# Columns of the activation tiles in SBUF, and the first weight panel of an encoder step

## The reference

```python
for l in range(DEPTH):
    hn = rmsnorm(x, p['norm_mix_pre'][l])
    m = mixer_even(hn, ...) if l % 2 == 0 else mixer_odd(hn, ...)
    x = x + rmsnorm(m, p['norm_mix_post'][l])
    hn = rmsnorm(x, p['norm_ffn_pre'][l])
    f = jnp.square(jax.nn.relu(hn @ p['mlp_up'][l])) @ p['mlp_down'][l]
    x = x + rmsnorm(f, p['norm_ffn_post'][l])
```

## Time and profile before

| | |
|---|---|
| median of 3 runs | 2187.01 us (2185.21 to 2187.84) |
| the profiled execution | 2186.56 us |
| its span, first to last instruction | 2184.6 us |
| TensorE busy | 2168.7 us, 99% |
| VectorE busy | 907.4 us, 42% |
| ScalarE busy | 666.8 us, 31% |
| TensorE's granted clock over the span | 0.998 |

### The profile page before, as it was taken

One profiled execution on the slowest core, in us unless ns is written; L12 is line 12 of the kernel. 1 busy time (PEld: TensorE's weight loads), 2 busy tenths in 40 slices (PEclk: granted clock), 3 DMA queues, 4 the chain that ended last, 5 costly groups with the idle time before them and its releaser, 6 DMA issues.

```text
span 2184.6 us, 31823 instructions
## 1 busy us (share of the span) xinstructions
PE 2168.7 (99%) x13629; PEld 2154.2 (99%) x13629; DVE 907.4 (42%) x1431; ACT 666.8 (31%) x1137; POOL 96.3 (4%) x115
## 2 busy tenths in 40 slices
PE   9999999999999999999999999999999999999998
PEld 8999999999999999999999999999999999999997
DVE  5766358323322322334953333493223223322336
ACT  6664345202311320333511112453013103202333
POOL 1000000000000000000033231000000000000000
PEclk9999999999999999999999999999999999999999
DMA  6111422111111111132311114221111111111132
GB/s 218 49 41 39 138 75 83 49 47 41 49 49 49 41 48 49 49 110 67 119 49 41 47 49 138 69 81 56 49 42 47 49 49 47 41 49 49 55 122 80
DMA packets 228891, 142.99 MB, mean 65 GB/s; under 512 B 5248, under 2 KB 227408, under 8 KB 228752
## 3 DMA queue, kind: packets, MB, share of 16 engines
q1 hardware_dynamic: 228304, 140.89, 21.3%
q0 software_dynamic: 416, 0.07, 0.0%
q10 hardware_dynamic: 32, 0.01, 0.0%
HBM read 119.22 MB, written 21.73 MB: 65 GB/s over the span
## 4 chain that ended last, share of the span: by engine, by line
PE 88%; DVE 2%; issue 0%; ACT 0%; DVEq 0%; ACTq 0%
PE ps L679 29%; PE ps L680 29%; PE ps L682 29%; DVE x_lo L1383 1%; DVE x_old L1372 0%; DVE f L1355 0%; PE ps L781 0%; DVE f L1339 0%; DVE f L1347 0%; DVE f L1365 0%; DVE w_all L1306 0%; PE ps L719 0%; DVE f L1434 0%; ACT tmp L945 0%; PE ps L804 0%
## 5 line engine op out<-in xcount | busy, mean ns | idle before, releaser
L679 PE MATMUL ps<-x_hi,w_all 128*128 128x352 f32 x2328 | 757.6, 325 | 1.5 <-DVE x_lo L1383 1.5
L680 PE MATMUL ps<-x_lo,w_all 128*128 128x352 f32 x2328 | 748.5, 322 | 0.0
L682 PE MATMUL ps<-x_hi,w_all 128*128 128x352 f32 x2304 | 740.3, 321 | 0.0
L679 PE MATMUL ps<-h_hi,w_all 128*128 128x352 f32 x1728 | 556.5, 322 | 0.0
L682 PE MATMUL ps<-h_hi,w_all 128*128 128x352 f32 x1728 | 555.2, 321 | 0.0
L680 PE MATMUL ps<-h_lo,w_all 128*128 128x352 f32 x1728 | 555.2, 321 | 0.0
L679 PEld LDWEIGHTS ps<-x_hi,w_all 128*128 128x128 f32 x2328 | 437.5, 188 | 5.4 <-issue 2.0
L680 PEld LDWEIGHTS ps<-x_lo,w_all 128*128 128x128 f32 x2328 | 437.6, 188 | 2.2
L682 PEld LDWEIGHTS ps<-x_hi,w_all 128*128 128x128 f32 x2304 | 432.6, 188 | 0.0
L909 ACT CAST w_all<-w_all_raw 128x1024 fp32r<-128x1024 f32 x168 | 175.5, 1045 | 522.1 <-DMA w_all_raw<-in_mlp_down_dram 317.8
L679 PEld LDWEIGHTS ps<-h_hi,w_all 128*128 128x128 f32 x1728 | 324.4, 188 | 0.4 <-DVE h_lo L1595 0.3
(11 more groups left out here) (218 smaller groups left out, 1458.0 us busy)
## 6 DMA issues: line engine op xcount, KB each, us to landing
w_all_raw<-in_mlp_up_dram SPq DMA_DIRECT2D x60, 512.0 KB, 3.9
w_all_raw<-in_mlp_down_dram SPq DMA_DIRECT2D x60, 512.0 KB, 3.9
x_save<-f SPq DMA_DIRECT2D x12, 1408.0 KB, 6.4
x_old<-x_save SPq DMA_DIRECT2D x12, 1408.0 KB, 11.5
w_all_raw<-in_c_w_in_dram SPq DMA_DIRECT2D x22, 512.0 KB, 3.8
w_all_raw<-in_w_in_even_dram SPq DMA_DIRECT2D x15, 512.0 KB, 3.8
x_rows<-in_x_prompt_dram SPq DMA_DIRECT2D x8, 512.0 KB, 7.5
w_all_raw<-in_w_out_even_dram SPq DMA_DIRECT2D x6, 512.0 KB, 3.9
```

The source lines that it names most:

```text
L679: nc.tensor.matmul(dst, wh, hi, start=(i == 0), stop=False)
L680: nc.tensor.matmul(dst, wh, lo, start=False, stop=False)
L682: last = nc.tensor.matmul(dst, wl, hi, start=False, stop=(i == KC - 1))
```

## The change

1. A chunk of x now has 1152 columns (`XS`), and its tiles stand 384 columns apart (1536 bytes, six times 256) with a gap of 32 columns behind each. All three tiles of x begin at the same place within 256 bytes, the one where tile 0 was. Tiles of h stay as they were.
2. The buffer `sq_sum` goes. Its 352 columns a tile lie in the gaps of x, as 11 pieces of 32 columns; so do `fold`, `root`, `rcol` and, in 4 pieces a row, `tail_rows`. VectorE's operations on them take the pieces in one instruction each.
3. `rstd` now stands behind `tmp` and is what the warm-up reads. Room that `sq_sum` gave is taken by what shared it: `bias_bc`, `v_tok_s` and `row_junk` lie on `tmp`; `xc1` and `ig1` lie in chunks 1 and 2 of `h_lo`, the scratch `v_junk` and `v_out_s` in chunk 3. So in `spatial_bias` the wait for the recurrence's last product and gates comes before step 3 and not 6, the wait for the output of v before step 9 and not 3, and `out_sum` waits for neither `v_out` nor `t_out`.
4. The first panel is loaded in two transfers, chunks 0 to 3 and 4 to 7. VectorE casts chunks 0 to 3; ScalarE casts chunks 4 to 7 as before.

```diff
+XS = TOK + 96
-        x_hi = place("x_hi", [P, KC * TS], F32R)
+        x_hi = place("x_hi", [P, KC * XS], F32R)
-        x_lo = place("x_lo", [P, KC * TS], F32R)
+        x_lo = place("x_lo", [P, KC * XS], F32R)
-        sq_sum = place("sq_sum", [P, TOK], F32)
+        gap_hi, gap_lo = [b[:, :].rearrange("p (g n) -> p g n", g=NT * KC)[:, :, TT:TT + QUAD] for b in (x_hi_raw, x_old)]
+        sq_sum = (gap_hi[:, 0:NJ], gap_hi[:, NJ:2 * NJ], gap_lo[:, 0:NJ])
+        fold = [gap_lo[:, NJ + i, 0:NJ] for i in range(6)]
+        def tile_at(buf, t):
+            return t * (TT + QUAD if buf.shape[1] == KC * XS else TT)
         def pt(buf, c, t):
-            c0 = c * (buf.shape[1] // KC) + t * TT
+            c0 = c * (buf.shape[1] // KC) + tile_at(buf, t)
...
+                elif l == 0:
+                    src = source(l).rearrange("(k p) n -> p k n", p=P)
+                    sp.dma_start(W[l][2][:, 0:4, :], src[:, 0:4, :]).then_inc(w_first, 16)
+                    sp.dma_start(W[l][2][:, 4:8, :], src[:, 4:8, :]).then_inc(w_in[slot], 16)
...
@@ ScalarE, start
-            act.wait_ge(w_in[LOADS[0].slot], 16)
-            nc.scalar.copy(W[0][0][:, 0:4, :], W[0][2][:, 0:4, :]).then_inc(w_half, 1)
             act.wait_ge(x0_a, 3)
             act.wait_ge(x0_b, 3)
             act.wait_ge(c_ok, 1)
             x_part(0, 0, 0, 4)
+            act.wait_ge(w_in[LOADS[0].slot], 16)
             nc.scalar.copy(W[0][0][:, 4:8, :], W[0][2][:, 4:8, :]).then_inc(w_high, 1)
@@ VectorE, start
             for n in range(3):
                 x_half(n)
+            dve.wait_ge(w_first, 16)
+            nc.vector.tensor_copy(W[0][0][:, 0:4, :], W[0][2][:, 0:4, :]).then_inc(w_half, 1)
             dve.wait_ge(x0_a, 3)
             x_low(0, 0, 0, 8)
+            dve.wait_ge(w_half, 1)
             low(0)
@@ spatial_bias
                 if n == 3:
+                    dve.wait_ge(lru_mul, 3 * 3 + 3)
+                    dve.wait_ge(gate_pe, 24)
+                if n == 9:
                     dve.wait_ge(v_out, 16)
-                if n == 6:
-                    dve.wait_ge(lru_mul, 3 * 3 + 1)
-                    dve.wait_ge(gate_pe, 24)
```

More of the change, by code:

```diff
@@ L240, in build @@
         row_rstd = place("row_rstd", [P, 9], F32)
-        x_hi_raw = place("x_hi_raw", [P, KC * TS], F32, at_x_hi)
-        x_old = place("x_old", [P, KC * TS], F32, at_x_lo)
+        x_hi_raw = place("x_hi_raw", [P, KC * XS], F32, at_x_hi)
+        x_old = place("x_old", [P, KC * XS], F32, at_x_lo)
         h_hi_raw = place("h_hi_raw", [P, KC * TS], F32, at_h_hi)
         h_lo_raw = place("h_lo_raw", [P, KC * TS], F32, at_h_lo)
-        spare = [x_hi_raw[:, k * TS + TOK:k * TS + TOK + NJ] for k in range(KC)]
-        fold, root, rcol = spare[0:6], spare[6], spare[7]
+        gap_hi, gap_lo = [b[:, :].rearrange("p (g n) -> p g n", g=NT * KC)[:, :, TT:TT + QUAD] for b in (x_hi_raw, x_old)]
+        sq_sum = (gap_hi[:, 0:NJ], gap_hi[:, NJ:2 * NJ], gap_lo[:, 0:NJ])
+        fold = [gap_lo[:, NJ + i, 0:NJ] for i in range(6)]
+        root, rcol = gap_lo[:, NJ + 6, 0:NJ], gap_lo[:, NJ + 7, 0:NJ]
+        tail_rows = gap_lo[0:T_COLS, NJ + 8:NJ + 12, :]
         x_rows = place("x_rows", [P, SEQ // P, D], F32, at_h_lo)
@@ L283, in build @@
                 cy.append(place(f"cy{n}{i}", [P, TOK], F32, at + 2 * TOK * 4 + 2 * c_step + i * TOK * 4))
-        v_out_s = place("v_out_s", [DEC, HALF], F32, at_h_lo + 8192)
-        tail_rows = place("tail_rows", [T_COLS, P], F32, at_sq)
+        v_out_s = place("v_out_s", [DEC, HALF], F32, at_h_lo + 13056 + HALF * 4)
         def chunk_buf(bufs, c):
@@ L369, in build @@
         warm = sem("warm")
+        w_first = sem("w_first")
         w_half = sem("w_half")
@@ L486, in out_piece @@
             n = P if s < 2 else TT - 2 * P
-            rows = part(x_old, 0, KC, t, s * P, s * P + P) if s < 2 else tiles3(x_hi_raw)[:, :, t * P:t * P + P]
+            rows = part(x_old, 0, KC, t, s * P, s * P + P) if s < 2 else tiles3(x_hi_raw)[:, :, (0, P, XS // NT)[t]:(0, P, XS // NT)[t] + P]
             return t, s * P, n, rows
@@ L789, in warm_up @@
             def warm_up(a):
-                nc.tensor.matmul(ps[:, a, 0:TT], tmp[0][:, 0:P], tmp[0][:, :], start=True, stop=True)
+                nc.tensor.matmul(ps[:, a, 0:TT], rstd[:, 0:P], rstd[:, 0:TT], start=True, stop=True)
             def keep_warm(a):
@@ L1255, in _ @@
                     act.wait_ge(t_pe, 1)
-                    nc.scalar.copy(tail_rows[:, :], ps[0:T_COLS, M0, 0:P]).then_inc(t_ok, 1)
+                    nc.scalar.copy(tail_rows, ps[0:T_COLS, M0, 0:P].rearrange("r (g p) -> r g p", p=QUAD)).then_inc(t_ok, 1)
                 if n == BLOCK[3] + 10:
@@ L1373, in x_sum @@
                     dve.wait_ge(x_tree, n + i + 1)
-                nc.vector.tensor_tensor(sq_sum[:, t * TT:(t + 1) * TT], pt(x_old, 0, t), pt(x_old, 1, t), ALU.add
-                                        ).then_inc(x_acc, 1)
+                a, c = [pt(x_old, k, t).rearrange("p (j c) -> p j c", c=QUAD) for k in range(2)]
+                nc.vector.tensor_tensor(sq_sum[t], a, c, ALU.add).then_inc(x_acc, 1)
                 rs_fold(u - 1, "pre", t)
```

35 lines of the change are left out of this document (14 added, 21 removed).

## The result

The changed kernel took 2200.19 us (median of 6 runs, 2199.64 to 2200.74) against 2186.25 us before (6 runs, 2185.21 to 2187.84): a ratio of 1.0063, 95% interval 1.0052 to 1.0074. It is slower by 13.9 us. The forecast, 2182.4 us, was wrong, and so was its range; what happened is rival D. Later runs add a second surprise: the same kernel, run ten times more, took 2187 to 2200 us, in steps.

A forecast was written before the change was run, and what follows sets the result against it. TensorE, busy 99%, was taken to bound the kernel by its matmul pace; 3.86 + 0 + 0.4 + 0.1 = 4.36 us saved, put at 4.4, gave a forecast of 2182.4 us, range 2180.8 to 2185.2.

The forecast's parts named there:

- rival D: Runs of x, chiefly the odd mixer: a 4.00 us rhythm lasts without tile 1; 8.2 us slower, 2195.2; chance 0.06.
- The bound: Whole kernel: TensorE busy 99%, so only the matmuls' pace or a wait removed at either end moves the time.
- Tiles of x in one place: 104 units of x's tile 1 each gain 0.04 us: 4.16, less 0.30 swallowed by waits, so 3.86 us.
- Sums in the gaps: VectorE's operations on 32-column pieces: taken to cost nothing, at most 0.55 us more each.
- the delay at its tile 2: Turn into the third phase: TensorE waits for `x_low` of tile 2, losing the 0.16 us gained by four tile 1 units.
- C: Third phase's turn and the end: VectorE's piece writes give time back; 2.45 us gained, 2184.6; chance 0.12.
- First panel: Start: `x_low` and unit 0 come 0.46 us earlier, 0.15 if a GpSimd select delays the cast; taken as 0.4 us.
- The clock: Start, TensorE's stretch at 0.50 clock: earlier work gains 0.23 us, up to 0.9 if no fall; taken as 0.1.
- E: Start: the clock stays up, 0.9 us more gained, 2181.5; chance 0.17.
- Rival B: Units of x: place does not set the pace, only the start gains 0.5 us, 2186.5; chance 0.05.

The follow-up runs named there:

- the fast version: Changed kernel with ident and quads back at their old place, plus one small quads matmul at the ninth unit of phases 2 to 4: 2182.39 us, ratio 0.9981.

## Why the prediction was wrong, point by point

- **The bound** was right: TensorE is at 99% before and after, and the pace decided all. The added time is in the pace of its matmuls, at full clock, and not in a wait.
- **Tiles of x in one place** is the step that failed. It says: "All of x's tiles get the place of tile 0", and takes 104 x 0.04 from the time, as if that place had the one pace 3.80. The 3.80 came true (first timeline above), and where nothing was slow it gave its due: -0.96 us in each stretch of 120 MLP units, 24 of them x's tile 1, at 0.04. But 3.80 is one of two rhythms of that place, and 4.00 us is the other: the odd mixer's 63 units took 252.36 us in place of 240.74, and at its fast level the same program took 239.8. Tile 1's units had been a protection that cost 4.2 us, and they went with the change. "What tile 1 has of its own is its place" holds for this kernel, but only because nearly all panels stand at one place; it is the place against the panel's that sets the pace.
- **Rival D** had this mechanism, with 12.6 us for 63 units; 11.62 was measured against the kernel before, whose own tile 1 is in the difference. It got 0.06 on one piece of evidence against it: a unit at 3.80 us one unit behind an interruption. That was one throw, at `quads`' old place; in the changed kernel the same unit takes 4.00. One fast case can't show that a persistent slow one is not started elsewhere, and rows 6 had shown a unit at 4.00.
- **What was not priced**: the new place of `ident` and `quads`. The change puts `rstd` ahead of them; nothing in the order or the counts shows that. It made 4.53 us at the turns. In the kernel before the move alone costs 0.7 to 0.8 us a turn (35.87, against 35.05 and 35.17), since tile 1 ends it. The prediction read the place of the moving operand from the trace and then did not ask which other operands had moved.
- **Sums in the gaps**: the value of nothing stands for the adds and folds (521 to 525 and 545 ns, as before). The copy costs 0.13 us more, twelve times, within the bound of 0.55 and hidden. The third turn took 0.12 us more than the others before (35.17 and 35.05); in the fast version it takes 0.26 more (35.15 and 34.89), so the delay at its tile 2 grew by 0.14 us, where 0.16 was worked out. C, the giving back, did not show.
- **First panel**: 0.46 us was worked out and 0.43 measured at unit 0. The cast took 0.48 us, was done at 10.32, 0.35 us ahead of `x_low`, and was not held by GpSimd, whose selects ran from 8.43 to 11.45. The prediction says that no row shows a VectorE copy beside GpSimd; rows 7 show one, the third copy at 8.46, but out of PSUM. By the rule of the Trainium skill in "SBUF — State Buffer", "Who interferes with whom", it could have waited for one; this trace does not show it. The 0.43 us are not resolved in the run times: the part alone measured 0.9998.
- **The clock**: E came true in the windows, 1.00 in place of 0.50, in the changed kernel and with the first panel alone. One profile each would not show that the earlier start did it, as the clock stayed up too in the profiles of two kernels with the old start (the layout alone, and `quads` moved in the kernel before). The runs do. With the old start the granted clock of the whole span is 0.998, as in the profile of before with its stretch at 0.50, in 31 of 88 runs of the kernel before, 5 of 10 with `quads` moved and 2 of 10 with the layout alone; with the new start it is 0.999 or more in all 93 comparable runs. (Every profile also has a stretch at 0.50 at its end, so this figure tells of the start only roughly.) The prediction gave that a chance of 0.17. For its size, the kernel before takes 0.9, 1.2 and 1.5 us longer at the median where it has 0.998, in three sets of runs on three chips. In the profiles the first 48 units of the first panel alone gained 0.92 us although the third copy came 0.68 later, 1.60 in all; 0.47 of that is the panel, which leaves 1.1 for the clock. The changed kernel's gained 0.69 with the copy 0.77 later; less 0.64 for 16 units of tile 1 and 0.43 for the panel that leaves 0.4, so one profile's remainder is no measure of it.
- **Rival B**, that place sets no pace, falls: moving all of x by 128 bytes made the odd mixer's units 3.87 us. The Trainium skill's "TensorE: Matmul & The Clock Gate", "Wait — 56ns, not 53.3ns?", gives start to start as columns over 2.4 GHz and some 2.5 ns, here 149 ns by an estimate. Measured were 158.3, 160.0, 161 and 166.7 ns for 352 columns, by place and rhythm; no run here shows 149.

The repeated runs lie on levels. That is why the first comparison, 13.9 us slower, is too large as a mean: at its lowest level the changed kernel takes 2187 us, at its highest 2200, and neither is the forecast. With `quads` back and one small matmul it is 2182.4.

**What stays open**: by what rule an interruption picks one rhythm or the other. A few ns at the second matmul behind a wait mostly go with it, but what sets these is not in the trace. Why the slow rhythm exists at all, and why `quads`' place matters, is shown only as an effect. Nor does the place decide alone: in the changed kernel the column sums of unit 70 left the slow rhythm, those of unit 68 did not (unit 69 took 3.81 us). At residue 0 `quads` stands at one place with `fold`, the moving operand of the column sums, and at 160 it does not. Whether that is the point is untested; the one run that moved `fold` against `quads` is the one that moved all of x, where no 4.00 could follow in x. Nor is it known whether the fast version holds on every chip and launch: nine of nine comparable runs here, on one chip.

## What to carry to other kernels

Where TensorE never waits, measure the pace by starts, over every long run of units, and look for more than one value at the same place; a unit that takes longer than its neighbours may be what ends a worse rhythm, so its cost is not simply its excess. When a buffer is resized, list what moves behind it, small stationary operands too, and pin each one's place within 256 bytes, a moving tile's against its panel's. Where one program's times lie in steps, six runs on one level are one sample: run it again elsewhere before a ratio is believed.

## What the runs showed of the hardware that was not expected

- A 352-column matmul of this kernel follows the last by 158.3 or 166.7 ns where its moving tile and its panel stand 128 bytes apart within 256 bytes, and by 160.0 or 161 ns where they stand at one place, all at a granted clock of 1.00. Moving the panel by 128 bytes, with the tile left where it was, turned 3.80, 3.84 and 3.80 us a unit into 3.84, 3.81 and 3.84.
- The 4.00 us rhythm lasted over 63 units, 1512 matmuls, and over changes of bank, panel and buffer. It is drawn anew at waits and sometimes at small or single matmuls in between, and in the profiles a whole unit at the panel's own place ended it each time. It also began and ended with no wait where a unit's tile and panel changed places together.
- The place of a 128 by 128 stationary operand used for 11 columns (residue 160 or 0 within 256 bytes) went with nine 352-column units behind it taking 34.89 or 36.60 us. What lies behind that operand moved with it.
- A VectorE copy of 352 columns takes 385 ns into one piece and 516 ns into eleven pieces of 32 columns; adding and folding cost the same either way (521 and 545 ns).
